# Setup order, squares pre-added for the router, norm roots by logarithm and exponential, and the last expert sum from its high half, in a two-model decoder kernel

## The reference

```python
def rms_norm(x, gain):
    y = xf * lax.rsqrt(jnp.mean(xf * xf, axis=-1, keepdims=True) + NORM_EPS)

# experts (first model): 8 groups of 4; the second: 4 groups of 8, expert width 512
group_w, group_id = lax.top_k(softmax(xt @ w_group), 1)
in_group = (xt @ w_router)[the chosen group]
top_logits, local_id = lax.top_k(in_group, 2)
gates = group_w * softmax(top_logits)
y = sum over the two experts of  gates * (silu(x @ w_gate[e]) * (x @ w_up[e])) @ w_down[e]
```

## Time and profile before

| | us |
|---|---|
| median of 3 runs | 2543.15 (2542.11 to 2546.96) |
| the profiled execution | 2540.95 |
| its span, first to last instruction | 2539.1 |
| TensorE busy, products | 2054.7 (81%) |
| VectorE, ScalarE busy | 637.7 (25%), 376.2 (15%) |
| read from device memory | 776.75 MB, 306 GB/s over the span |

### The profile page before, as it was taken

One profiled execution on the slowest core, in us unless ns is written; L12 is line 12 of the kernel. 1 busy time (PEld: TensorE's weight loads), 2 busy tenths in 40 slices (PEclk: granted clock), 3 DMA queues, 4 the chain that ended last, 5 costly groups with the idle time before them and its releaser, 6 DMA issues. The chain is left out here.

```text
span 2539.1 us, 33840 instructions
## 1 busy us (share of the span) xinstructions
PE 2054.7 (81%) x14308; PEld 1302.4 (51%) x14309; DVE 637.7 (25%) x1483; ACT 376.2 (15%) x808; POOL 76.6 (3%) x104
## 2 busy tenths in 40 slices
PE   7898778898777999999966666689989998666665
PEld 5574336574334688888622222238888883222222
DVE  5452103551112236364200000022541121000001
ACT  1431001431002022200100000011211010000000
POOL 0201000101000000000000000000000000000000
PEclk9999989999888999999987888899999999888788
DMA  9359999355999332198899999973312369999996
GB/s 387 139 232 382 428 428 401 133 226 240 429 428 408 112 137 101 60 387 346 329 428 429 429 428 428 428 315 116 149 36 100 133 271 428 427 428 429 428 428 284
DMA packets 55842, 779.36 MB, mean 307 GB/s; under 512 B 6840, under 2 KB 7096, under 8 KB 8120
## 3 DMA queue, kind: packets, MB, share of 16 engines
q1 hardware_dynamic: 55736, 777.82, 73.6%
HBM read 776.75 MB, written 1.05 MB: 306 GB/s over the span
## 5 line engine op out<-in xcount | busy, mean ns | idle before, releaser
L1967 PE MATMUL bank<-ring,xnT 128*32 128x512 f32 x3136 | 480.4, 749 | 308.2 <-DMA ring<-in_w_exp 307.9
L1967 PEld LDWEIGHTS bank<-ring,xnT 128*32 128x32 f32 x3136 | 101.1, 124 | 675.0 <-DMA ring<-in_w_exp 356.3
L1992 PE MATMUL bank<-ring,arena 128*32 128x512 f32 x1440 | 174.2, 621 | 73.1 <-DMA ring<-in_w_exp 38.8
L971 PE MATMUL bank<-xnT,ring 128*128 128x256 f32 x960 | 210.7, 379 | 0.0
L2163 DVE TENSOR_TENSOR arena<-bank,arena 128x256 f32<-128x256 f32 (+1 forms) x33 | 18.3, 553 | 718.3 <-PE bank L1967 517.4
L971 PEld LDWEIGHTS bank<-xnT,ring 128*128 128x128 f32 x960 | 181.6, 190 | 28.4 <-issue 4.5
L1657 PE MATMUL bank<-xnT,ring 128*128 128x256 f32 x768 | 173.6, 379 | 0.0
L1657 PEld LDWEIGHTS bank<-xnT,ring 128*128 128x128 f32 x768 | 146.1, 190 | 22.1 <-issue 2.5
L1926 PE MATMUL bank<-arena,xnT 128*128 128x256 f32 x592 | 144.5, 399 | 3.6 <-DVE xnT L2174 3.6
L1926 PEld LDWEIGHTS bank<-arena,xnT 128*128 128x128 f32 x592 | 114.7, 199 | 62.8 <-issue 47.8
L1992 PEld LDWEIGHTS bank<-ring,arena 128*32 128x32 f32 x1440 | 48.3, 112 | 174.7 <-issue 72.5
(11 more groups left out here) (435 smaller groups left out, 2050.0 us busy)
## 6 DMA issues: line engine op xcount, KB each, us to landing
ring<-in_w_exp SPq DMA_DIRECT2D x274, 2048.0 KB, 25.7
arena<-in_w_ada SPq DMA_DIRECT2D x24, 2048.0 KB, 11.6
ring<-in_w_in SPq DMA_DIRECT2D x20, 2048.0 KB, 25.9
ring<-in_w_merge SPq DMA_DIRECT2D x18, 2048.0 KB, 8.2
arena<-in_w_exp SPq DMA_DIRECT2D x14, 2048.0 KB, 15.0
ring<-in_w_o SPq DMA_DIRECT2D x8, 2048.0 KB, 11.7
ring<-in_w_conv SPq DMA_DIRECT2D x6, 2048.0 KB, 8.0
ring<-in_w_rest SPq DMA_DIRECT2D x2, 1696.0 KB, 25.5
```

What stands on the lines that cost most here:

```text
L971: last = nc.tensor.matmul(o[:, T * j:T * j + T], w[:, k, col:col + P], xnT[:, k, :], start=k == 0, stop=k == KT - 1)
L1967: last = nc.tensor.matmul(o[rows(e), :], Xw[:, k, rows(e)], w[:, at:at + MW], start=k == 0, stop=k == KT - 1)
L1992: last = nc.tensor.matmul(o[rows(e), :], hidT[:, j, rows(e)], w[:, at:at + MW], start=j == 0, stop=j == ft - 1)
```

## The change

Four edits and what they bring along:

1. **Setup order.** x is the first transfer, then the constants (on a semaphore of their own), the positions, the layer's vectors, c and `vecg`. The Silu of c and the four sines leave `setup`; a new function `sines` runs them on ScalarE at the start of `project1` of layer 0, and VectorE waits for it after the scaling of x.
2. **Norm.** `preload_act_table(Sqrt)` becomes the table with logarithm and exponential; the root becomes `Ln`, then a wait of ScalarE on it, then `Exp` with scale -0.5 in place. VectorE's reciprocal (`norm_rstd`) is gone at all six places.
3. **Router.** The squares of slices 0 to 5 are added on VectorE (slices 2 and 3 onto 0 and 1, then 4 and 5, then 1 onto 0), behind its adds of slices 4 and 6 to `hT`. One-column products remain for that sum and for slices 6 and 7. The router products of slice 6 are issued inside the last product group, behind its k = 5.
4. **End of moe.** `combine` for slices 4 to 7 waits only for `y1_taken`; then slices 0 to 3. Adds, squares and sums follow in the order of pairs 2, 3, 0, 1.

```diff
+        def sines(act, c_ready):
+            for w, tab in enumerate((rope_tab, ret_tab)):
+                nc.scalar.activation(tab[:, 0], ang2[:, w, :, 0:half[w]], ACT.Sin)
+                nc.scalar.activation(tab[:, 1], ang[:, w, :, 0:half[w]], ACT.Sin)
+            act.wait_ge(c_loaded, 32)
+            nc.scalar.activation(c_all, c_all, ACT.Silu).then_inc(c_ready, 1)
...
-                    sp.dma_start(cst[:], dram["consts"]).then_inc(in_loaded, 16)
                     sp.dma_start(hT[:], dram["x"]).then_inc(x_loaded, 16)
-                    sp.dma_start(vecg[:], dram["vecg"]).then_inc(in_loaded, 16)
+                    sp.dma_start(cst[:], dram["consts"]).then_inc(cst_loaded, 16)
                     sp.dma_start(pos_i[:, 0:TT], dram["positions"]).then_inc(in_loaded, 16)
                     sp.dma_start(pos_i[:, TT:2 * TT], dram["positions_2"]).then_inc(in_loaded, 16)
+                    vectors_early(sp, 1, 0, 0)
                     sp.dma_start(c_all, dram["c_row"]).then_inc(c_loaded, 16)
-                    vectors_early(sp, 1, 0, 0)
+                    sp.dma_start(vecg[:], dram["vecg"]).then_inc(c_loaded, 16)
...
+        PAIRS = (2, 3, 0, 1)
...
-            nc.scalar.preload_act_table(ACT.Sqrt)
-            for q in range(4):
+            nc.scalar.preload_act_table_set("natural_log_exp_and_others")
+            for i, q in enumerate(order):
                 if not known:
-                    act.wait_ge(added, 2 * q + 2)
+                    act.wait_ge(added, 2 * i + 2)
                 nc.scalar.activation(sq[:, 2 * q:2 * q + 2, :], hT[:, 2 * q:2 * q + 2, :], ACT.Square).then_inc(sq_ready, 1)
             act.wait_ge(sum_ready, 1)
-            nc.scalar.activation(rstd, b[:, 0:T], ACT.Sqrt, scale=1.0 / D, bias=EPS).then_inc(root_ready, 1)
+            nc.scalar.activation(rstd, b[:, 0:T], ACT.Ln, scale=1.0 / D, bias=EPS).then_inc(root_ready, 1)
+            act.wait_ge(root_ready, 1)
+            nc.scalar.activation(rstd, rstd, ACT.Exp, scale=-0.5).then_inc(root_ready, 1)
...
+        def route_squares_sum(pe, sems, sq, nr, d):
+            if d == 0:
+                pe.wait_ge(sq_added, 3)
+            else:
+                pe.wait_ge(sq_ready, d - 2)
+            for t in range(TT):
+                last = nc.tensor.matmul(bank[4][:, 2 * nr + t:2 * nr + t + 1], sq[:, d, P * t:P * t + P], K("ones")[:, 0:1], start=False, stop=d == KT - 1, skip_group_check=True)
...
+        def route_squares_add(dve, sems, sq, q):
+            dve.wait_ge(sems[1], q + 1)
+            if q == 2:
+                dve.wait_ge(sq_added, 1)
+            nc.vector.tensor_tensor(sq[:, 0:2, :], sq[:, 0:2, :], sq[:, 2 * q:2 * q + 2, :], ALU.add).then_inc(sq_added, 1)
+            if q == 2:
+                dve.wait_ge(sq_added, 2)
+                nc.vector.tensor_tensor(sq[:, 0, :], sq[:, 0, :], sq[:, 1, :], ALU.add).then_inc(sq_added, 1)
...
+                                if n == 5 and j == 3 and k == 5:
+                                    route_sums(pe, norms, wr1, nr1, range(6, 7), True)
...
-                    route_sums(pe, norms, sq, wr1, nr1, range(6, 8), True)
+                    route_squares_sum(pe, norms, sq, nr1, 0)
+                    route_squares_sum(pe, norms, sq, nr1, 6)
+                    route_sums(pe, norms, wr1, nr1, range(7, 8), True)
+                    route_squares_sum(pe, norms, sq, nr1, 7)
...
                     pe.wait_ge(y1_taken, n_items + 1)
+                    combine(sum_ready, range(4, 8))
                     pe.wait_ge(y0_taken, n_items + 1)
-                    combine(sum_ready)
-                    norm_sums(pe, norms, bank[4])
+                    combine(sum_ready, range(4))
+                    norm_sums(pe, norms, bank[4], PAIRS)
```

More of the change, by code:

```diff
@@ L336, in norm_sems, with norm_squares, norm_sums @@
             return tuple(sem(f"{tag}_{n}") for n in ("added", "sq", "sum", "root"))
-        def norm_squares(act, sems, b, known=False):
+        PAIRS = (2, 3, 0, 1)
+        def norm_squares(act, sems, b, known=False, order=range(4)):
             added, sq_ready, sum_ready, root_ready = sems
-            nc.scalar.preload_act_table(ACT.Sqrt)
-            for q in range(4):
+            nc.scalar.preload_act_table_set("natural_log_exp_and_others")
+            for i, q in enumerate(order):
                 if not known:
-                    act.wait_ge(added, 2 * q + 2)
+                    act.wait_ge(added, 2 * i + 2)
                 nc.scalar.activation(sq[:, 2 * q:2 * q + 2, :], hT[:, 2 * q:2 * q + 2, :], ACT.Square).then_inc(sq_ready, 1)
             act.wait_ge(sum_ready, 1)
-            nc.scalar.activation(rstd, b[:, 0:T], ACT.Sqrt, scale=1.0 / D, bias=EPS).then_inc(root_ready, 1)
-        def norm_sums(pe, sems, b, ks=range(KT)):
+            nc.scalar.activation(rstd, b[:, 0:T], ACT.Ln, scale=1.0 / D, bias=EPS).then_inc(root_ready, 1)
+            act.wait_ge(root_ready, 1)
+            nc.scalar.activation(rstd, rstd, ACT.Exp, scale=-0.5).then_inc(root_ready, 1)
+        def norm_sums(pe, sems, b, order=range(4)):
             added, sq_ready, sum_ready, root_ready = sems
[L352 to L362, removed]
+            for i, q in enumerate(order):
+                pe.wait_ge(sq_ready, i + 1)
+                for k in (2 * q, 2 * q + 1):
+                    last = nc.tensor.matmul(b[:, 0:T], K("ones"), sq[:, k, :], start=k == 2 * order[0], stop=i == 3 and k % 2 == 1)
+            last.then_inc(sum_ready, 1)
         def norm_scale(dve, scaled, gain, dest):
@@ L472, in _ @@
                 def _(act):
+                    if l == 0:
+                        sines(act, c_ready)
+                        act.wait_ge(c_ready, 1)
                     for b in (0, 2, 4, 6):
@@ L1922, in gather, with combine @@
                         last.then_inc(high_gathered, 1)
-                    def combine(ready=None):
-                        for d in range(KT):
+                    def combine(ready=None, ds=range(KT)):
+                        for d in ds:
                             last = nc.tensor.matmul(bank[d // 2][:, T * (d % 2):T * (d % 2) + T], Yw[:, P * d:P * d + P], gwT, start=False, stop=ready is not None, skip_group_check=True)
@@ L2053, in _ @@
                     item(n_items - 1, False)
-                    norm_squares(act, norms, bank[4])
+                    norm_squares(act, norms, bank[4], order=PAIRS)
                 @block.gpsimd
@@ L2179, in _ @@
                     item(n_items - 1, False)
-                    for d in range(KT):
-                        dve.wait_ge(sum_ready, d // 2 + 1)
+                    for i in range(KT):
+                        d = 2 * PAIRS[i // 2] + i % 2
+                        dve.wait_ge(sum_ready, i // 2 + 1)
                         y = bank[d // 2][:, T * (d % 2):T * (d % 2) + T]
@@ L2187, in _ @@
                         last.then_inc(norms[0], 1)
-                    norm_rstd(dve, norms)
         def next_layer(last_used):
```

68 lines of the change are left out of this document (35 added, 33 removed).

## The result

The changed kernel took 2508.45 us (median of 4 runs, 2506.02 to 2509.56), the kernel before 2545.06 beside it: ratio 0.9857, 95% interval 0.9838 to 0.9877. Timed again, it gave 2507.86 and the same ratio [0.9831, 0.9883]. The profiled execution took 2506.02, its span is 2504.2.

A forecast was written before the change was run, and what follows sets the result against it. Transfers pace the expert loops, one chain of TensorE, ScalarE and VectorE the rest; 4.7 + 3.5 + 6.7 - 1.3 + 10.7 = 24.3 us saved gave 2516.6, or 2518.9 on the runs' median scale; range 2511 to 2527.

The forecast's parts named there:

- Setup, 4.7: Setup, once: TensorE starts the first projection at 18.8 and not 23.5, 4.7 us saved.
- End of the expert stages and root, 3.5 + 6.7: Four expert stage ends: high half first saves 3.5 us; five norms: logarithm and exponential replacing root and reciprocal save 6.7.
- Load that came back, 1.3: Latents' root in layer 1's attention stage: a table load returns there, 1.3 us lost.
- Router, 10.7: Four routers: fewer one-column products and slice 6's router products moved earlier save 2.7 us each, 10.7 in all.
- Passed on: Expert stages: transfers start earlier with TensorE's progress, so time saved ahead of them still counts.
- The clock: Rival, chance 0.27: three falls of TensorE's clock beside changed places vanish, 5 us more, 2513.8.
- The range: Whole kernel: 2511 to 2527 us, taking in clock gain and some loss, setup's bounds and the runs' spread.
- the trace agrees: TensorE's clock: the trace was said to bear out the skill's claim that throttled is the default and activity releases it.

The follow-up runs named there:

- after_table: The changed kernel with the table for the latents' root loaded early, in model 1's first projection: 2503.08 us, ratio 0.9835 to the kernel before.
- before_wide: The kernel before with the router's one-column products made 128 columns wide: 2538.56 us, ratio 0.9981.
- before_warm: The kernel before with 10 unread spare products behind the norm sums of each of the four expert stages: 2533.52 us, ratio 0.9957.
- router_only: The kernel before with the router edits alone: 2525.63 us, ratio 0.9921.
- the norm pair: The kernel before with root by logarithm and exponential and the last expert sum from its high half: 2530.63 us, ratio 0.9952.
- after_again: The changed kernel, unaltered, timed and profiled a second time: 2507.86 us, ratio 0.9857 to the kernel before.
- before_again: The kernel before, unaltered, profiled a second time: 2549.49 us, a single run.
- after_all_warm: The changed kernel with 128-column products, early root table, and spare products ahead of the latents' transposes and behind expert norm sums: 2497.13 us, ratio 0.9808.

## Why the prediction was wrong

- **Setup, 4.7.** Right in the trace: start at 19.12 (18.8 forecast), 4.4 earlier than before, and VectorE's last copy of the projection 4.8 earlier. In time it is worth 3.3 inside the whole and 0.5 alone; 4.7 is just outside the interval of the second, [-3.6, 4.6], and well inside that of the first.
- **End of the expert stages and root, 3.5 + 6.7.** Right: 2.28 against 2.21 at the place shown. From the last copy to the root the first three expert stages take 8.88 before and 7.93 after, 0.95 against 0.88.
- **Load that came back, 1.3.** Right, and it is on the path in layer 0 too: after_table took both away.
- **Router, 10.7.** Right as work: 31.75 - 29.18 = 2.6, and 34.24 - 31.60 = 2.6 in the second model, where both sides are at full clock. That is 10.3 for the four.
- **Passed on.** Right: the expert stages take 1334.5 us against 1332.8, so they gave back at most 1.7.
- **The clock: this step failed.** The prediction kept it out of the sum, as a rival at 0.27 worth 5 us, because "new falls may appear". The runs show that it belonged in the sum, with some 10 us. Kept up behind the narrow products, with no work removed, it is worth 5 us [0.5, 9] (before_wide), kept up in the norms' pauses 11 [7, 15] (before_warm); router_only brought 9 over its own term, the norm pair 3 over its own. The rival had the mechanism and the sign; it counted three vanishing falls out of ten. By the pooled traces the routers' clock is worth 5.6 us and the norms' 4.8, together 10.4 of the 12 that were missing. In the two profiles shown, stage by stage, what exceeds the terms is: 3.2 at the second model's two routers; 2.9 from the last copy to the last root (11.73 against 7.93), where the kernel before was at low clock for 6.6 us; 1.9 and 2.4 between the second model's norms and its routers; 0.8 and 0.7 in the first model; less some 1.7 in the expert stages. The routers' part is shown to hang on the narrow products, since widening them removes it. The norms' part hangs on the pause: filling it does in the one profile what shortening it does in eight, and the time bears it out. For the last combine and for the attention and merge stages no run tells the edit's part from chance: after_again has a low stretch of 17 us there (1869 to 1886) and ends at the same time all the same.
- **The range.** Its low end, 2511, held the gaining clock's 2513.8 and little more. Three falls was one choice out of ten; all ten gone would have been 17 us, and that end was left out.

What stays open: whether the setup edit alone is really worth less than its term. Its profile has a plain reading (ten microseconds at 1.2 GHz at the first router), but before_again shows the same stretch with no edit, so this may be chance. That the norm edits measured low alone and high together is within their intervals. And why the second model has falls behind its roots in all five profiles with the changed routers is not known.

## What to carry to other kernels

Where TensorE is the bound between waits, price an edit twice: its instructions, and the falls of the granted clock that stand behind the narrow products or the pause it removes, 1.7 us each here, and each weighed by how often it is there. The cheapest test is to fill: widen one-column products that are bound by their weight loads anyway, or put unread products in a norm's pause. Here that alone, with no work removed, gave 5 and 11 us. Take several profiles of the kernel before ahead of counting falls: the second model's last router alone had none, one or two in eight of them, and all four routers together had 2 to 5.

## What the runs showed of the hardware

- The granted clock fell behind one-column products though TensorE shows no idle time. Windows of the kernel before, ahead of the 0.50 of the earlier trace rows:

```profile
1200.00:1202.00 2.00, 2.00 (x20) 2.00 (x20) 0.20 (x1) 0.47 (x1) 0.00 (x0) 1.00 1.02 434
...
1202.00:1204.00 2.00, 2.00 (x16) 1.92 (x16) 0.00 (x0) 0.00 (x0) 0.00 (x0) 0.97 0.99 418
```

  Ahead of the 8 one-column instructions there stand 26 of 36 columns; with only those 8 made 128 columns wide the clock stays at 1.00 (before_wide). The Trainium skill, "TensorE: Matmul & The Clock Gate", section "Part 1: The HAM clock gate", says that the clock is set by how busy TensorE has been recently. This trace doesn't bear that out if "busy" is read as the profile's busy time, which is 2.00 of 2.00 us in both windows. So the prediction's "the trace agrees" holds for 176:178 and 408:410 in the earlier trace rows, which stand behind pauses, and not for 1204:1206.
- Wide is nearly free: 128 columns instead of 1 changed the router stretch by 0.1 us (31.75 to 31.85; 29.18 to 29.29).
- Products with a constant matrix of ones on both sides, read by nobody, kept the clock up as well: in after_all_warm the 34 instructions ahead of the latents' transposes (75.6 to 79.7), and the up-projection behind them, are at 1.00, where the changed kernel is at 0.50 for 10 us.
- The logarithm of 128x256 out of PSUM takes 0.38 and the exponential out of SBUF 0.42, 0.41 from start to start, against 1.75 for VectorE's reciprocal of the same shape.
